# The second block's first feed-forward product, taken as seven half-size products per couple of tiles

## The reference, cut to what matters

```python
def sq_relu_mlp(h, w1, w2):
    return jnp.square(jax.nn.relu(h @ w1)) @ w2

h2 = modulate_2(rms_norm_2(x, norm2_g[l]), sh2, sc2)
x = x + g2 * sq_relu_mlp(h2, w_ff1[l], w_ff2[l])
```

## Time and profile before

| what | value |
|---|---|
| timed runs | 1749.98, 1751.79, 1760.3 us |
| median of the runs | 1751.79 us |
| span of the profiled execution | 1751.2 us |
| its instructions | 21311 |
| PE busy, share of the span | 1693.3 us, 97% |
| DVE, ACT, POOL busy | 713.3 us, 319.7 us, 0.2 us |

### The profile page before, as it was taken

How to read it: one execution, slowest core, us unless ns; L and a number is a source line. 1 busy time by engine, 2 the same in 40 slices (tenths; PEclk the granted TensorE clock), 3 DMA queues, 4 the chain that set the end, 5 groups by cost and what they waited for, 6 DMA issues and landing times. The chain is left out here.

```text
span 1751.2 us, 21311 instructions
## 1 busy us (share of the span) xinstructions
PE 1693.3 (97%) x8962; PEld 1217.1 (69%) x8962; DVE 713.3 (41%) x1519; ACT 319.7 (18%) x711; POOL 0.2 (0%) x4
## 2 busy tenths in 40 slices
PE   5999999999999999999999999999999999999997
PEld 4674887887663567676667667688855677788654
DVE  4467884526025220111011055644565445421554
ACT  4210013103114111010000034521100135111000
POOL 0000000000000000000000000000000000000000
PEclk8999999999999999999999999999999999999998
DMA  9665887466899999999999994136774232244410
GB/s 373 287 240 194 351 350 303 179 240 247 337 386 407 414 421 421 421 421 421 421 421 421 421 403 156 73 125 260 288 306 174 96 121 94 99 144 157 159 68 24
DMA packets 62375, 474.82 MB, mean 271 GB/s; under 512 B 7783, under 2 KB 11272, under 8 KB 12616
## 3 DMA queue, kind: packets, MB, share of 16 engines
q1 hardware_dynamic: 61048, 472.18, 67.6%
q10 hardware_dynamic: 1232, 1.28, 0.2%
HBM read 472.38 MB, written 1.05 MB: 270 GB/s over the span
## 5 line engine op out<-in xcount | busy, mean ns | idle before, releaser
L2642 PE MATMUL bank<-hT,ring 128*128 128x256 f32 x928 | 200.6, 379 | 0.0
L2642 PEld LDWEIGHTS bank<-hT,ring 128*128 128x128 f32 x928 | 176.3, 190 | 24.0
L1381 PE MATMUL bank<-hT,ring 128*128 128x256 f32 x704 | 160.7, 385 | 4.2 <-issue 2.8
L1381 PEld LDWEIGHTS bank<-hT,ring 128*128 128x128 f32 x704 | 132.9, 191 | 38.5 <-issue 14.5
L679 PE MATMUL bank<-hT,ring 128*128 128x256 f32 x704 | 152.6, 379 | 0.0
L679 PEld LDWEIGHTS bank<-hT,ring 128*128 128x128 f32 x704 | 133.8, 190 | 19.5 <-issue 1.4
L1850 PE MATMUL bank<-ring,rowsT 128*32 128x512 f32 x1008 | 117.7, 600 | 0.0
L2613 PE MATMUL bank<-ring,second_work 128*128 128x512 f32 x192 | 97.1, 592 | 0.0
L1381 PE MATMUL bank<-tmp,ring 128*128 128x256 f32 x384 | 86.5, 382 | 1.9 <-DMA ring<-in_w_ff 1.3
L1381 PEld LDWEIGHTS bank<-tmp,ring 128*128 128x128 f32 x384 | 71.9, 190 | 20.5 <-issue 7.5
L3072 DVE TENSOR_TENSOR second_work<-second_work 128x256 f32<-128x256 f32 x64 | 26.8, 424 | 127.4 <-ACT second_work L2825 127.4
(11 more groups left out here) (505 smaller groups left out, 2117.9 us busy)
## 6 DMA issues: line engine op xcount, KB each, us to landing
ring<-in_expert_w SPq DMA_DIRECT2D x190, 1024.0 KB, 15.7
ring<-in_w_ff SPq DMA_DIRECT2D x64, 1024.0 KB, 9.5
ring<-in_ada_wT SPq DMA_DIRECT2D x22, 2048.0 KB, 10.4
ring<-in_w_ff_pairs SPq DMA_DIRECT2D x32, 1024.0 KB, 4.9
ring<-in_w_in SPq DMA_DIRECT2D x29, 1024.0 KB, 6.7
ring<-in_ada_w SPq DMA_DIRECT2D x14, 2048.0 KB, 13.5
ring<-in_w_in SPq DMA_DIRECT2D x13, 2048.0 KB, 9.2
ring<-in_w_out SPq DMA_DIRECT2D x12, 1024.0 KB, 8.2
```

What stands on the lines that cost most here:

```text
L1381: mm = pe.matmul(ctx_bank(i)[:, 0:T], w, x, start=part == n == 0, stop=part == parts - 1 and n == len(products) - 1)
L2642: mm = pe.matmul(ff_bank(n), w[:, k, (n % 2) * P:(n % 2 + 1) * P], hT[:, k, xs], start=k == 0, stop=k == DT - 1)
```

## The change

Of the 32 tiles of each layer, tiles 0 to 3 stay as they are. The other 28 form 14 couples (2 to 15), a couple being one weight chunk. A couple's product of 256 features by 256 tokens over 1024 inputs is split 2x2: two halves of the inputs (4 of the 8 k each), two feature tiles, two halves of the tokens. Seven products of 128 features by 128 tokens over 4 k replace the eight.

- GpSimd makes four sums of weight quarters per couple (`up_summed`), each 128x512; one of them in place in the ring.
- DVE makes four sums of token quarters once per layer (`token_summed`).
- PE runs 28 half-width matmuls per couple (`up_couple`) into two banks, even couples in banks 4 and 5, odd ones in 0 and 1.
- ACT copies the first product out of PSUM, DVE makes four combinations (`combined`), and ACT applies Relu and Square to both tiles at once (`couple_squared`), so DVE's 32 squarings go.
- The late chunks are spread: four in the first layer's first product, one in its second product, two in the second layer's first product. Their 28 steps follow: 14 behind the couples of layer 0, 6 behind steps 2 to 7 of its second product, 8 behind couples of layer 1.
- The sums of the second product's steps 0 and 1 move behind couples 14 and 15. `windowed(1)` and the modulation bias move into the second product.

The diff, cut to its core:

```diff
+            late = [features_first("ada_wT_2_1", j) for j in LATE_CHUNKS]
+            beside = [late[0:4], late[5:7]][l]
             plan_both(f"ff1_{l}", [wide("w_ff1_2", j, l, n=GW) for j in range(16)], beside,
-                      [int(j % 2 == 1 and j // 2 < len(beside)) for j in range(16)])
+                      [int(j % 4 == 1 and j // 4 < len(beside)) for j in range(16)])
+            beside = [late[4:5], []][l]
...
+            UP_SEVEN = (("A11", "B11"), ("A12", "B21"), ("S2", "T2"), ("S4", "B22"), ("S1", "T1"), ("S3", "T3"), ("A22", "T4"))
+            UP_AT = (0, 1, 2, 3, 5, 6, 4)
...
+                    def up_couple(l, p):
+                        wait_chunk(pe, at[f"ff1_{l}"][p])
+                        if p == FIRST_COUPLE + 1:
+                            pe.wait_ge(S("ff1_out"), WHOLE_TILES * (l + 1))
+                        if p >= FIRST_COUPLE + 2:
+                            pe.wait_ge(S("up_combined"), coupled(l, p - 2))
+                        q = token_quarters() | up_quarters(l, p)
+                        for n, (w, x) in enumerate(UP_SEVEN):
+                            if n == 2:
+                                pe.wait_ge(S("up_sums"), UP_SUMS * coupled(l, p))
+                                if p == FIRST_COUPLE:
+                                    pe.wait_ge(S("token_sums"), TOKEN_SUMS * (l + 1))
+                            for k in range(4):
+                                mm = pe.matmul(up_bank(p, UP_AT[n]), q[w][:, k, :], q[x][:, k, :], start=k == 0, stop=k == 3)
+                            if n == 3:
+                                mm.then_inc(S("up_first"), 1)
+                        mm.then_inc(S("up_couple"), 1)
...
-                        for n in range(FT):
+                        for n in range(WHOLE_TILES):
...
+                        for p in range(FIRST_COUPLE, FT // 2):
+                            up_couple(l, p)
...
+                    def up_summed(l, p):
+                        wait_chunk(pool, at[f"ff1_{l}"][p])
+                        if p >= FIRST_COUPLE + 2:
+                            pool.wait_ge(S("up_couple"), coupled(l, p - 2))
+                        else:
+                            pool.wait_ge(S("norm_sum"), 2 * l + 1)
+                            pool.wait_ge(S("out_tile"), DT * (l + 1))
+                        nc.gpsimd.tensor_tensor(q["S1"], q["A21"], q["A22"], ALU.add).then_inc(S("up_sums"), 1)
+                        pool.wait_ge(S("up_sums"), before + 1)
+                        nc.gpsimd.tensor_tensor(q["S2"], q["S1"], q["A11"], ALU.subtract).then_inc(S("up_sums"), 1)
+                        nc.gpsimd.tensor_tensor(q["S3"], q["A11"], q["A21"], ALU.subtract).then_inc(S("up_sums"), 1)
+                        pool.wait_ge(S("up_sums"), before + 2)
+                        nc.gpsimd.tensor_tensor(q["S4"], q["A12"], q["S2"], ALU.subtract).then_inc(S("up_sums"), 1)
...
+                    def couple_squared(l, p):
+                        h = W[:, 2 * p:2 * p + 2, :]
+                        act.wait_ge(S("up_combined"), coupled(l, p))
+                        nc.scalar.activation(h, h, ACT.Relu).then_inc(S("up_relu"), 1)
+                        act.wait_ge(S("up_relu"), coupled(l, p))
+                        nc.scalar.activation(h, h, ACT.Square).then_inc(S("ff_ready"), 1)
...
+                        for p in range(FIRST_COUPLE, FT // 2):
+                            act.wait_ge(S("up_first"), coupled(l, p))
+                            nc.scalar.copy(first_product(p), up_bank(p, 0)).then_inc(S("up_first_out"), 1)
+                            if p > FIRST_COUPLE:
+                                couple_squared(l, p - 1)
...
+                    def token_summed(l):
+                        dve.wait_ge(S("h"), 16 * l + DT)
+                        tt(q["T1"], q["B12"], q["B11"], ALU.subtract).then_inc(S("token_sums"), 1)
+                        tt(q["T3"], q["B22"], q["B12"], ALU.subtract).then_inc(S("token_sums"), 1)
...
+                        tt(q["T2"], q["B22"], q["T1"], ALU.subtract).then_inc(S("token_sums"), 1)
+                        tt(q["T4"], q["B21"], q["T2"], ALU.subtract).then_inc(S("token_sums"), 1)
+                    def combined(l, p):
+                        dve.wait_ge(S("up_first_out"), coupled(l, p))
+                        all_of(dve, tt(pair(low), both(first_product(p)), pair(up_bank(p, 1, 2)), ALU.add))
+                        dve.wait_ge(S("up_couple"), coupled(l, p))
+                        all_of(dve, tt(pair(carried), both(low[:, P:2 * P]), pair(up_bank(p, 5, 2)), ALU.add))
+                        tt(pair(high), both(carried[:, P:2 * P]), pair(up_bank(p, 4, 2)), ALU.add)
+                        tt(low[:, P:2 * P], carried[:, 0:P], up_bank(p, 3), ALU.add).then_inc(S("up_combined"), 1)
...
-                        for n in range(FT):
-                            dve.wait_ge(S("ff1_out"), FT * l + n + 1)
-                            tt(W[:, n, :], W[:, n, :], W[:, n, :], ALU.mult).then_inc(S("ff_ready"), 1)
...
+                        token_summed(l)
+                        for p in range(FIRST_COUPLE, FT // 2):
+                            combined(l, p)
+                            if p + 2 >= FT // 2:
+                                sums(l, p + 2 - FT // 2)
...
+                            if l == 0:
+                                late_weigh(p - FIRST_COUPLE)
+                            if l == 1 and LATE_SECOND + p - FIRST_COUPLE < len(late_steps):
+                                late_weigh(LATE_SECOND + p - FIRST_COUPLE)
```

More of the change, by code:

```diff
@@ L2320, in build @@
             ff_shift = sb("ff_shift", [P, 4], second)
+            late_chunks = at["ff1_0_beside"] + at["ff2_0_beside"] + at["ff1_1_beside"]
             late_steps = [(n, i) for n in range(len(LATE_CHUNKS)) for i in range(4)]
+            LATE_FIRST, LATE_SECOND = 16, 20
             RAW_TILES = 3
[L2323 removed]
+            WHOLE_TILES = RAW_TILES + 1
+            FIRST_COUPLE, COUPLES = WHOLE_TILES // 2, FT // 2 - WHOLE_TILES // 2
+            UP_SUMS, TOKEN_SUMS, HIDDEN_READY = 4, 4, 1 + COUPLES
+            token_sums = sb("token_sums", [P, 2 * HEADS, P], second)
             x_raw = W[:, 22:31, :].rearrange("p a t -> p (a t)")[:, 0:DT * (T + 1)].rearrange("p (k n) -> p k n", n=T + 1)
@@ L2391, in build, with token_quarters, up_quarters, up_bank @@
             C11, C12, C22, C21 = quad
+            quarter = lambda x, k, h: x[:, 4 * k:4 * k + 4, h * P:(h + 1) * P]
+            of_quarters = lambda x: x.rearrange("p (k t) -> p k t", k=4)
+            def token_quarters():
+                h = hT[:, :, xs]
+                held = cT[:, 4:8, :].rearrange("p (i a) t -> p i (a t)", i=2)
+                return {"B11": quarter(h, 0, 0), "B12": quarter(h, 0, 1), "B21": quarter(h, 1, 0), "B22": quarter(h, 1, 1),
+                        "T1": of_quarters(held[:, 0, :]), "T2": of_quarters(held[:, 1, :]),
+                        "T3": token_sums[:, 0:4, :], "T4": token_sums[:, 4:8, :]}
+            def up_quarters(l, p):
+                w = chunk_tile(at[f"ff1_{l}"][p], GW)
+                S1, S2, S4 = [of_quarters(tmp[:, 4 * (p % 2) + i, :]) for i in range(3)]
+                return {"A11": quarter(w, 0, 0), "A12": quarter(w, 1, 0), "A21": quarter(w, 0, 1), "A22": quarter(w, 1, 1),
+                        "S1": S1, "S2": S2, "S3": quarter(w, 0, 1), "S4": S4}
+            UP_SEVEN = (("A11", "B11"), ("A12", "B21"), ("S2", "T2"), ("S4", "B22"), ("S1", "T1"), ("S3", "T3"), ("A22", "T4"))
+            UP_AT = (0, 1, 2, 3, 5, 6, 4)
+            def up_bank(p, i, n=1):
+                b = (bank[4], bank[5]) if p % 2 == 0 else (bank[0], bank[1])
+                return b[i // 4][:, (i % 4) * P:(i % 4 + n) * P]
+            first_product = lambda p: tmp[:, 4 * (p % 2) + 3, 3 * P:4 * P]
+            carried = tmp[:, 7, 0:2 * P]
+            def coupled(l, p):
+                return COUPLES * l + p - FIRST_COUPLE + 1
+            def hidden_ready(l, n):
+                return HIDDEN_READY * l + (1 if n < WHOLE_TILES else n // 2 - FIRST_COUPLE + 2)
             def added_squares(norm):
@@ L2714, in _ @@
                     load_biases(1)
-                    load_ahead(sp, at["ff2_1"][0] + 15)
+                    load_ahead(sp, at["ff2_1"][-1])
                     store(sp)
+                @block.gpsimd
+                def _(pool):
+                    def up_summed(l, p):
+                        q = up_quarters(l, p)
+                        before = UP_SUMS * (coupled(l, p) - 1)
+                        wait_chunk(pool, at[f"ff1_{l}"][p])
[10 more added lines that the diff above has]
+                        nc.gpsimd.tensor_tensor(q["S4"], q["A12"], q["S2"], ALU.subtract).then_inc(S("up_sums"), 1)
+                    for l in range(LAYERS):
+                        for p in range(FIRST_COUPLE, FT // 2):
+                            up_summed(l, p)
                 @block.scalar
@@ L3005, in late_weigh @@
```

(2 more changed lines are left out.)

72 lines of the change are left out of this document (41 added, 31 removed).

## The result

The changed kernel took 1738.33 us in the median of 6 runs (1734.63 to 1741.58), the kernel before 1751.19 beside it: ratio 0.9921, 95% interval 0.9902 to 0.9939. That is 12.9 us faster, less than the 1% (17.5 us) by which the prediction told faster from the same, and 0.3 us from the forecast. The profiled execution took 1734.63 us, its span is 1732.8.

A forecast was written before the change was run, and what follows sets the result against it. The prediction took columns streamed through PE as the bound. From a span of 1751.2 us, minus 18.7 for shorter records, plus 4.8 for the seam, it got 1737.3, so a 1738 us median; range 1732 to 1757.

The forecast's parts named there:

- the seam: Ahead of tile 3, GpSimd's first sums take turns with DVE's eight `scaled`: 2.4 us lost per layer, 4.8 in both.
- PE's records: Couples' matmuls: 784 half-width records at 111.4 ns, 87.4 us per layer instead of 96.7, gaining 18.7 us in two layers.
- GpSimd's sum: Each weight sum in the couples placed at 1.1 us, hidden behind PE up to 1.5 us, costing nothing.
- The cover: In each couple with a late step, GpSimd needs 5.8 us, under PE's 6.24 us.
- rival A: At the seam, DVE and GpSimd take no turns or sums are short: full gain, 1733.1 us; chance 0.26.
- The loads of couples 8 and 12: Chunks waiting for late steps still land in time for GpSimd's sums: taken as 0 us of PE waiting.
- The step to the second product: Sums of its steps 0 and 1, moved behind couples 14 and 15, finish before PE needs them: no cost.
- Rival B: Throughout the couples GpSimd becomes the bound, 4g + 0.2 us per couple (g per sum): 1762 us at 1.8; chance 0.16.
- Rival C: Couples' narrow records run slower in a long row, at 135.6 ns: 1776 us; chance 0.08.
- The turns: At the seam, DVE instructions with two SBUF inputs and GpSimd's sums exclude each other for a whole instruction.

The follow-up runs named there:

- experiment 8: Changed kernel without weight sums, couples' matmuls streaming half the token columns, then loading half the weight columns: 111.6 and 109.3 ns a record; 1737.36 and 1729.05 us.
- experiment 2: Changed kernel with two waits making GpSimd hold back its sums until DVE's eight `scaled`, then its token sums, are done: 1729.08 us, again 1731.76 us.
- experiment 5: Changed kernel, GpSimd's order kept, with the eight `scaled` reading one of their two tensors from PSUM: 1729.83 us, again 1730.69 us.
- experiment 6: Changed kernel with GpSimd making the first of its four sums twice, five instructions per couple: 1762.84 us, ratio 1.0058 to the kernel before.

## Why the prediction was right

The time came out 0.3 us from the forecast, and the terms of the sum hold one by one. Without the seam's loss a layer gains 111.44 - 102.30 = 9.14 us (forecast 9.35); the seam takes 2.30 of it (forecast 2.4).

- **PE's records.** Forecast 111.4 ns from the bursts of L1835, 87.4 us a layer. Measured 112.0 on the chain, 111.7 where nothing disturbs, 87.54 us. The reason given, that the load sets the pace, is at most half of it: experiment 8 shows that without half of the load the pace stays within 2.3 ns.
- **GpSimd's sum.** Placed at 1.1 us, undisturbed 1.27, with 1.23 from start to start. The Trainium skill's figure (GPSIMD Engine Reference, section 3.1), quartered to 1.12 us, is an estimate that came 0.15 short. The cover was forecast at 5.8 of 6.24 us with a late step; where GpSimd runs freely the trace has 1231.36 - 1225.46 = 5.90:

```profile
1225.46 1.26 POOL L2797 TENSOR_TENSOR tmp<-ring 128x512 f32<-128x512 f32 x1
1226.80 2.14 POOL L2799 TENSOR_TENSOR tmp<-tmp,ring 128x512 f32<-128x512 f32 x1
...
1231.36 1.26 POOL L2797 TENSOR_TENSOR tmp<-ring 128x512 f32<-128x512 f32 x1
```

- **The seam.** Forecast: five sums between the `scaled`, which then last 9.4 us; tile 3 late by 1.6, 0.8 of waiting for token sums, 2.4 together. Measured: 9.36 us; 1.74 late, the couple's third product 0.5 later, 2.30 together by experiment 2. This term was the choice between forecast and rival A, and experiment 5 shows the mechanism behind it. That its size fits so closely is partly luck: with the measured 1.27 us a sum the forecast's count, 0.7 us and five sums, gives 0.7 + 5 x 1.27 = 7.05 us of delay, not 6.2. In the trace the sum in progress and five more hold six of the eight `scaled`, and 9.36 - 3.25 = 6.11 us makes only 1.02 for each turn, less than a sum.
- **Nothing elsewhere.** The loads of couples 8 and 12 in layer 0 and of couple 8 in layer 1 kept GpSimd waiting 1.30 to 1.31 us each, unseen by PE; forecast 0. The step to the second product cost 0, as forecast. ACT and DVE stood nowhere else on the chain of these two stretches.
- **Rival A** (1733.1 us, no turns) is what experiments 2 and 5 made of the kernel: 1729 to 1732, a little below it.
- **Rival B** (GpSimd as the bound) did not come. Its formula fits layer 0 of experiment 6: 7.36 us a couple are, by 4g + 0.2, 1.79 us a sum, and the 100.66 us measured are the formula's 99.0 and the clock's 1.6. That the run took 1762.84 us, near the prediction's 1762 at 1.8 us a sum, is chance: in layer 1 only six of twelve couples are counted at that pace, and 3.2 us are the clock's.
- **Rival C** (narrow records slower in a long row) did not come: 0.3 to 0.6 ns more than in the short bursts.

That the total agrees to 0.3 us is partly luck. The profiled span is 4.5 us under the sum, ahead of anything that was changed, and the median of the runs stands 3.7 above that execution.

## What to carry to other kernels

Work given to an idle engine is free only where it doesn't meet the critical engine on a shared resource: look at where the new work starts, not only at whether its sum fits. Here two waits, or one operand moved to PSUM, brought back 2.3 us per layer that no count of busy time showed. And a margin of 0.3 us per couple is a bound in waiting: one instruction more turned a gain of 13 us into a loss of 10.

## What the runs showed of the hardware that was not expected

- The turns were forecast, the way out was not: beside GpSimd's sums, six of the eight `scaled` went from 0.48 to 1.48 us, and with one tensor in PSUM all kept 0.48. The combinations, with one operand in PSUM, keep 0.42 us too, while a late step, with two SBUF tensors, takes 1.86 us beside the sum of 2.14 shown above, in place of 1.22 and 1.27:

```profile
1225.41 0.42 DVE L3089 TENSOR_TENSOR second_work<-tmp,bank 128x256 f32<-128x256 f32 x1
...
1225.95 1.86 DVE L3141 SCALAR_TENSOR_TENSOR ring<-ring,cond_row 128x1024 f32<-128x1024 f32 x1
```

- A record with a 128x128 load and 128 columns keeps 109 to 112 ns when half its columns or half its weights are left out.
- PE's clock fell to the 1.2 GHz level in the middle of the couples (0.52 granted), behind a wait of 1.8 us, and that cost 1.6 us beyond the wait itself; behind four other waits of 1.7 to 1.8 us it did not fall.
